# The chunk mask of differential attention: mask products on TensorE against a VectorE memset in PSUM

## What is computed

```python
def _chunk_mask(q_pos, k_pos):
    return (k_pos[None, :] // CHUNK) <= (q_pos[:, None] // CHUNK)      # CHUNK = 64

def diff_fn(qs, qp):
    (qb,) = qs
    sc = jnp.einsum('bqhcd,bkhcd->bchqk', qb, dk_all).astype(jnp.float32) * DIFF_SCALE
    sc = jnp.where(_chunk_mask(qp, k_pos), sc, -jnp.inf)
    pr = jax.nn.softmax(sc, axis=-1)
    att = (pr[:, 0] - lam * pr[:, 1]).astype(dv_all.dtype)
    return jnp.einsum('bhqk,bkhd->bqhd', att, dv_all)
```

## Time and profile before

| what | value |
|---|---|
| median of three runs | 1057.7 us (1056.29 to 1058.37) |
| the profiled execution's own time | 1057.04 us |
| its span, from first to last instruction | 1055.2 us |
| PE busy | 909.0 us (86%) |
| DVE busy | 474.5 us (45%) |
| ACT busy | 365.1 us (35%) |
| POOL busy | 201.1 us (19%) |
| granted TensorE clock, mean | 0.936 of 2.4 GHz |
| stage b | from 338.8 us (first score product) to 426.2 us (last `gate_out`) |

### The profile page before, as it was taken

How to read it: one execution, slowest core, us unless ns; L and a number is a source line. 1 busy time by engine, 2 the same in 40 slices (tenths; PEclk the granted TensorE clock), 3 DMA queues, 4 the chain that set the end, 5 groups by cost and what they waited for, 6 DMA issues and landing times.

```text
span 1055.2 us, 12519 instructions
## 1 busy us (share of the span) xinstructions
PE 909.0 (86%) x4357; PEld 623.0 (59%) x4357; DVE 474.5 (45%) x1073; ACT 365.1 (35%) x851; POOL 201.1 (19%) x242
## 2 busy tenths in 40 slices
PE   6899999999998899997679798827997787777898
PEld 6887878787876676454457586823332222223686
DVE  3463454637373799376866524151111011114552
ACT  3633434343343789523246224101111111114321
POOL 0231312121121000556910102001110101100000
PEclk9899999999999899998889699557999999999899
DMA  7234242422222310014011393619999999993511
GB/s 227 83 116 133 79 126 60 140 65 80 81 61 84 107 43 29 1 61 150 16 31 46 114 339 130 232 46 356 412 418 419 417 419 417 417 412 152 179 40 50
DMA packets 79042, 179.05 MB, mean 170 GB/s; under 512 B 15810, under 2 KB 31220, under 8 KB 78980
## 3 DMA queue, kind: packets, MB, share of 16 engines
q1 hardware_dynamic: 71556, 160.27, 42.0%
q0 software_dynamic: 7424, 17.98, 4.6%
HBM read 163.92 MB, written 21.64 MB: 176 GB/s over the span
## 4 chain that ended last, share of the span: by engine, by line
PE 35%; DMA 15%; DVE 6%; issue 2%; ACT 1%; SPq 0%; DVEq 0%; ACTq 0%; POOLq 0%
DMA raw_e<-in_w_ei 14%; PE acc L754 5%; PE acc L643 5%; PE acc L1347 5%; PE acc L1340 4%; PE acc L1450 2%; PE acc L659 2%; PE tp L1304 2%; PE acc L603 2%; PE acc L1411 2%; PE acc L726 1%; PE tp L1434 1%; DMA xg<-hn_rows,src_row 1%; PE tp L632 1%; PE acc L1336 1%
## 5 line engine op out<-in xcount | busy, mean ns | idle before, releaser
L1340 PE MATMUL acc<-whi,lhi 128*128 128x512 f32 (+2 forms) x448 | 177.0, 395 | 10.2 <-DVE wlo L1702 7.3
L1340 PE MATMUL acc<-wlo,lhi 128*128 128x512 f32 (+2 forms) x448 | 174.5, 390 | 0.0
L1340 PE MATMUL acc<-whi,llo 128*128 128x512 f32 (+2 forms) x448 | 174.3, 389 | 0.0
L643 PE MATMUL acc<-raw_e,xT 128*64 128x512 f32 x512 | 122.8, 612 | 35.4 <-DMA raw_e<-in_w_ei 34.6
L643 PEld LDWEIGHTS acc<-raw_e,xT 128*64 128x64 f32 x512 | 37.4, 140 | 117.8 <-issue 116.5
L1513 ACT ACTIVATE whi<-raw,gcol 128x512 fp32r<-128x512 f32 (+2 forms) x96 | 61.5, 689 | 124.8 <-issue 115.2
L1340 PEld LDWEIGHTS acc<-whi,lhi 128*128 128x128 f32 x448 | 86.1, 192 | 29.6 <-DVE wlo L1702 9.7
L1340 PEld LDWEIGHTS acc<-whi,llo 128*128 128x128 f32 x448 | 85.9, 192 | 17.6
L1340 PEld LDWEIGHTS acc<-wlo,lhi 128*128 128x128 f32 x448 | 86.0, 192 | 16.7
L1702 DVE SCALAR_TENSOR_TENSOR wlo<-raw,gcol,whi 128x512 fp32r<-128x512 f32 (+2 forms) x96 | 64.8, 717 | 51.6 <-ACT whi L1513 51.5
L2059 POOL TENSOR_TENSOR small<-small,neghalf 128x8 f32<-128x8 f32 (+2 forms) x46 | 68.9, 1497 | 3.8
(11 more groups left out here) (243 smaller groups left out, 1443.6 us busy)
## 6 DMA issues: line engine op xcount, KB each, us to landing
raw_e<-in_w_ei SPq DMA_DIRECT2D x128, 512.0 KB, 15.8
raw_e<-in_w_eo SPq DMA_DIRECT2D x64, 512.0 KB, 16.5
raw<-in_w_in SPq DMA_DIRECT2D x40, 512.0 KB, 3.6
raw<-in_w_out SPq DMA_DIRECT2D x8, 512.0 KB, 6.3
wp_raw<-in_w_ple_gate SPq DMA_DIRECT2D x8, 512.0 KB, 7.1
raw_e<-y_rows SPq DMA_DIRECT2D x4, 1024.0 KB, 8.2
va_rows<-raw POOLq DMA_DIRECT2D x12, 256.0 KB, 3.1
vh<-va_rows SPq DMA_DIRECT2D x8, 384.0 KB, 3.5
```

The lines of the kernel that those rows point to most:

```text
L643: mm = pe.matmul(acc[rows, 0, :], xT[:, 2 * c + k, rows], raw_e[:, slots[2 * c + b], 512 * k:512 * k + 512], start=(c == 0 and k == 0), st ...
L1340: mm = pe.matmul(bank, L[x][:, kk, rows], W[w][:, n, k, 0:c.width], start=(kk == 0 and x + w == 0), stop=(kk == c.kt - 1 and x == 1))
```

## The change

The two mask products of a unit are gone, and the score products end their accumulation themselves. In their place DVE writes -1e30 into the last 64 key columns of both maps for the first 64 queries, ahead of its reduction and with a `link` between the two. The `mask` tile, its clearing on POOL, its two loads on SP and SP's wait for `zeroed` ahead of them are gone, and the number of constants waited for falls from 19 to 17.

```diff
@@ trunk
-        mask = sb("mask", [P, P + CHUNK])
...
-        NCONST = 19
+        NCONST = 17
@@ sync
             sp.dma_start(rope[:, :, :], a["c_rope"].rearrange("(t p) n -> p t n", p=P)).then_inc(ld_const, 16)
-            sp.wait_ge(zeroed, 1)
-            for row in (0, DB):
-                sp.dma_start(mask[row:row + 1, :], a["c_mask"]).then_inc(ld_const, 16)
             sp.dma_start(gq_lat[:, :], a["g_q_lat"].partition_broadcast(P)).then_inc(ld_const, 16)
@@ tensor, scores
                             mm = pe.matmul(acc[0:ROWS[t], score_bank(ph, n, c), 0:nk], qT[dims, hd, q],
-                                           kT[dims, hd, k0:k0 + nk], start=True, stop=(t == PT))
-                        for c in range(maps if t < PT else 0):
-                            dims = slice(DB * c, DB * c + DB)
-                            mm = pe.matmul(acc[:, score_bank(ph, n, c), nk - CHUNK:nk], mask[dims, 0:P],
-                                           mask[dims, P:P + CHUNK], start=False, stop=True)
+                                           kT[dims, hd, k0:k0 + nk], start=True, stop=True)
                     mm.then_inc(s_done[ph], 1)
@@ vector, maxima
                     if n >= bank_uses(ph):
                         dve.wait_ge(exp_done[ph], maps * (n + 1 - bank_uses(ph)))
+                    if ph == "b" and t < PT:
+                        link(dve.memset(acc[0:CHUNK, b:b + maps, nk - CHUNK:nk], -BIG))
                     dve.tensor_reduce(negmax[0:rows, b:b + maps], acc[0:rows, b:b + maps, 0:nk], AX.X, ALU.max,
                                       negate=True).then_inc(nm_done[ph], 1)
@@ gpsimd
-            link(pool.memset(mask[:, :], 0.0))
```

## The result

| | before | after |
|---|---|---|
| median of the runs compared | 1056.94 us (20 runs, 1055.27 to 1058.57) | 1061.53 us (20 runs, 1057.36 to 1062.98) |
| profiled execution: own time, span | 1057.04, 1055.2 us | 1060.3, 1058.5 us |
| stage b in the trace, first to last DVE row | 87.88 us | 91.86 us |
| a head of stage b | 9.80 us | 10.52 us |

The changed kernel is slower: the ratio of its time to that of before is 1.0041, 95% interval 1.0032 to 1.0049, 3.4 to 5.2 us. In the trace the stage is 4.0 us longer. It is counted from the DVE addition that ends the products ahead of it (337.98 before, 338.93 after) to the last `gate_out` (425.86 and 430.79).

The account below looks back on a forecast made before the run. The prediction took DVE's list, 9.29 us of work in a 9.80 us head, as the bound. Six heads added 2.8 us, the first head took off 0.35: 2.5 us slower, 1060.0 us said, range 1056.5 to 1062.9.

Parts of the forecast that it names:

- What bounds the kernel: Stage b: DVE has 9.29 us of work in a 9.80 us head; the loop runs through PE, ACT and DVE.
- What the change removes: Stage b: 128 mask products off PE, giving back only DVE wait time, 0.16 + 0.29 = 0.45 us a head.
- The two waits of DVE: At tile 3 of a head: 0.16 us for the mask product, 0.35 us for the exponentials, 0.29 of it taken as saved.
- What it adds: Four memsets a head on DVE, each with a wait behind it: 0.23 us each, between 0.13 and 0.32.
- m: Time by which one memset moves DVE's reduction: 0.19 us row plus 0.04 us gap, 0.23 us taken.
- the memset starts where the reduction started: On DVE in stage b: the memset takes the reduction's old start, so only its row and a 0.04 us gap add.
- The sign that was named for it: Reduction starts about 0.23 us behind its memset's start; under 0.15 or over 0.3 us would make the forecast wrong.
- the forecast's own formula: Slowdown of the whole kernel: 6 x (4m - 0.45) + (m - 0.58) = 25m - 3.3 us.
- The first head and the end: Stage b's edges: first head's reduction 0.35 us earlier; nothing taken behind the last wide reduction.
- SP's queue and the clock: SP saves 0.73 us of issuing at the start, nothing taken; stage b's clock stays at 1.00, chance of falling 0.03.
- the cheap memset: Rival, memset to reduction on DVE: m = 0.13 or 0.11, sum 0.0 or -0.5 us, not slower; chance 0.25.
- The dear memset: Rival, memset on DVE at the reduction's price: m = 0.32, 4.7 us slower, 1062.4 us; chance 0.22.

Follow-up runs that it names:

- run 1: The changed kernel without its memset, so no mask in differential attention, against the kernel before: 1054.63 us against 1057.5, ratio 0.9971, head 9.59 us.
- run 8: The kernel before with its mask products kept and the change's memset added, against the kernel before: ratio 1.0037, head 10.53 us.
- runs 2 and 3: The changed kernel with its memset writing scratch in SBUF (ratio 1.0024), or only 2 elements a partition in PSUM (1.0014), each against the kernel before.

## Why the prediction was right, and where its sum was off

The direction and the range were right: 1060.0 us was said, 1056.5 to 1062.9, slower at a chance of 0.52; it was 1061.53. The sum was too small, 2.5 us against 4.0 in the trace and about 4.3 by the ratio.

- **What bounds the kernel** held: after the change DVE's list sets the head but for a gap of 0.08 us, PE and ACT wait for it, and no other wait came next.
- **What the change removes** was right for this change, and wrong as a price on its own. The two waits of DVE shrank by 0.16 and by 0.35 - 0.08 = 0.27 us; 0.45 was said. But run 1 shows that without the memsets only 0.21 of it is there, and run 8 that with them the products cost nothing. The condition "if DVE is not made later by anything else" stood the wrong way round: the second wait shrinks *because* DVE is made later. The forecast let the exponentials come forward and the maximum stay, though it had just moved the maximum forward by the first wait; by run 1 both move together. That the 0.43 came in the change is owed to the memsets, not to the reason given.
- **What it adds** is the step that failed, in its size: m was 0.30 us, not 0.23. The row was 0.165, a little less than the 0.19 that came from the slope of the reductions (the slope of the two memset rows, (92 - 60) / 38 = 0.84 ns, would have given 60 + 126 x 0.84 = 166 ns), and the gap behind it 0.03, not 0.04. What was missing is in the sentence "the memset starts where the reduction started": it starts 0.10 us later, and 0.10 + 0.165 + 0.03 is the 0.30. The sign that was named for it, a reduction 0.23 us behind the start of its memset, could not show this: it came as 0.19 to 0.20. The difference of 0.07 us makes 25 x 0.07 = 1.8 us in the forecast's own formula, and 25 x 0.30 - 3.3 = 4.2 us is what came.
- **The first head and the end.** The wide reduction that ends the first head came 0.59 us earlier after the start of the stage (16.77 against 17.36 us), where 0.35 was said; without any mask, in run 1, it came only 0.22 earlier. Over all the traces this stretch takes 16.0 to 17.8 us, 6.8 to 13.7 of them at a granted clock of 1.2 GHz, so the products' part of it isn't settled. Behind the last wide reduction the stage got 0.20 us longer (11.94 against 11.74), where nothing was taken. With the six heads between, 63.15 us instead of 58.78, 4.37 more, the stage adds up: 4.37 - 0.59 + 0.20 = 4.0.
- **SP's queue and the clock** did as taken: no gain at the start, 1.00 in the six heads.

Of the rivals the cheap memset fell. Its row is indeed cheap, but the start before it and the wait behind it are not: at 2 elements and a row of 0.06 us m is still 0.18. The dear memset, m = 0.32, was the nearest in price, though not for its reason, since the row is not the reduction's 0.28.

The two rules of the Trainium skill can be placed now. Its longer fixed part for PSUM (the Trainium skill, VectorE: DVE Perf Modes, section on the TRN2 errata), carried over to a write, gave an estimate of 258 ns and m = 0.30. The m is what came, but the row is 165 ns in PSUM and 0.17 us in SBUF as well, so the fixed part isn't in the row; what PSUM adds here is 0.05 us in the start. The statement that a semaphore between chained instructions costs nothing extra, which the Trainium skill makes of a chain of copies (VectorE: DVE Perf Modes, section on the DRAIN), does not hold for this pair, and the measurement decides: the reduction starts 0.03 us behind the memset's end, 0.11 later than one without a wait does, and m falls from 0.30 to 0.14 us when another instruction stands between the two.

What stays open is what holds the memset back by those 0.10 us: runs 2 and 3 part it into two halves and show that it hardly depends on the length, but name no cause.

## What to carry to other kernels

Before work is moved from one engine to another inside a loop, look whose instructions follow one another without a gap: what leaves the others is returned as waiting, and what comes to that one is paid in full, with its late start and the wait behind it, not by its row alone. Where a short operation sits on the engine that has waits, make it shorter there (here one pass instead of four). And when a buffer changes its size, look at the rates of the transfers into everything that is allocated behind it before the edit itself is judged.

## What the runs showed of the hardware that was not expected

- A DVE memset starts late: 0.02 us behind the end of the instruction ahead when it writes PSUM and 0.03 before it when it writes SBUF, where a reduction in its place starts 0.08 before it. Its row is 60 ns for 2 elements and 165 for 128, in PSUM and SBUF alike, 0.83 ns an element, less than the 1.02 of the reductions. A scaling that follows it without a wait has a row of 0.27 us instead of 0.35.
- From the start of a pair of 64-column mask products to the work behind it is 0.26 us in float32 and 0.12 in bfloat16; scores and a pair in one-pass float32 together take as long as with bfloat16 (1.10 and 1.09 us). A pair of 64 by 64 in float32 costs the full 0.26 as well.
- While the experts' weights are loaded, DMA moves 417 to 418 GB/s where their slots in SBUF lie 0, 256 or 768 bytes off the place they had in the kernel before (twelve traces), and at 409 to 410 where they lie 384 bytes off it (two traces).
